# Moving a key and value compression from its own block into the mixers' block of a decoder layer

## The chip, the cores and the metric

One NeuronCore of a Trainium2 chip runs one layer of a hybrid decoder. The metric is the device time of one execution in microseconds (us). TensorE is called PE, VectorE DVE, ScalarE ACT, GpSimd POOL and SyncE SP. Three timed runs of the kernel before stand behind its time, and one profiled execution behind its profile.

## What is computed

x has 2048 rows of 1024 channels. The layer normalises x, multiplies by W_in to get z (3096 columns), runs three groups of heads over z, multiplies the joined result by W_out, adds x, and ends with an MLP. The groups are a retention (4 heads of 64), a short gated convolution, and an attention of 8 heads in 2 key groups with three branches: compressed, selected and window. The change is about what feeds the compressed branch:

```python
def compress(t, pe, w1, w2):
    blocks = kv_heads(t)[:, win_idx] + pe[None, None, :, None, :]
    flat = blocks.transpose(0, 1, 3, 2, 4).reshape(b, n_cmp, G, CMP_LEN * d)
    return jax.nn.silu(flat @ w1) @ w2

k_cmp = rms_norm(compress(k_c, pe_k, w1_k, w2_k), k_gain)
v_cmp = compress(v_c, pe_v, w1_v, w2_v)
```

A window is 32 rows long and starts at every 16th row, so there are 127 of them; d is 64, so flat has 2048 columns and w1 is 2048 x 64. There are two kinds (keys and values) and two groups (G). Nothing of the compressed branch, the first in each tile's attention, can start before k_cmp is there.

## The kernel before

build_layer (L2012) issues five phases. Each is a block of its own: five instruction streams (SP, POOL, ACT, DVE, PE), each in its own fixed order, synchronised by semaphores, and all engines meet at the end of a block.

**projection_phase (L56)** computes z in two halves of 8 row tiles. In each half 9 column blocks of W_in are loaded by SP, split by ACT (split_hi, L160) and POOL into a high and a low part, and multiplied by PE. DVE copies the sums out and SP stores them to z_scratch in DRAM.

**compress_phase (L411)** is the compression. SP loads the identity, then kv, the 256 key and value columns of all 16 row tiles, in one DMA (L480); then it waits until DVE has cleared w1, w2 and pe_rows (L604 to L606), and loads the weights twice, once for each group's half of the partitions (L485 to L487), and then the constants that the mixers need. PE transposes kv in 32 pieces (L549), ACT copies them to kvT (L587). w1 is laid out block-diagonally as 128 x 128 for each of the 32 positions l, so that one matmul serves both groups: kind 0 takes 32 matmuls (L561), each with the 127 columns of kvT that start at l and lie 16 apart. Then the bias of both kinds, pe @ w1, takes 64 matmuls with one moving column (L569), then kind 1 takes its 32 (L561). SiLU is made by ACT and DVE, the second product is at L574, the keys are normalised with a square root on POOL (L536, L537), transposed (L579) and copied to cmp_k (L637). POOL meanwhile fills masks and constants (L503 to L533), and ACT writes the rows that mark the key blocks into ka_s (L590).

**mixers_phase (L758)** starts after that. The class Plan (L666) writes out one list of steps, and PE, ACT and DVE each go through it in this order, doing what is theirs. The list begins with prep(0), the preparation of tile 0 in 22 pieces (PIECES, L645), and goes on with prep(1) merged into the first attention steps. The pieces:

- "squares" (ACT), "sums" (DVE) and "gates" (DVE) read the loaded tile of z;
- "fill qq" to "fill q1" are work of PE into one PSUM bank, prep_ps, and each "read" empties it before the next "fill": qq and kz are transposes (L1298), scores 4 matmuls (L1302), output 12 matmuls (L1308 to L1310), k, q0 and q1 transposes (L1316);
- "normalise k", "normalise q", "high" and "low" are DVE and ACT work on the normalised queries and keys.

POOL has no list. For each tile it copies the values (L964, L967), makes the rotation (L977 to L986, which releases "fill qq"), the root for the normalisation (L993), the convolution taps (L998 to L1004), then waits for the retention's output and finishes it (L1007 to L1013), and only then begins the next tile. SP's load(i) (L914) brings tile i by five DMAs on one semaphore: z, two copies of columns shifted by one and two rows (L928; of tile 0 these have 127 and 126 rows), the rotation (L930) and a selection table (L931). The step "compressed" (L1318) is the first that needs cmp_k, and its first instruction is the mask matmul at L1322. output_phase and mlp_phase follow and are the same in both kernels.

An fp32 matmul of the program appears in the trace as two records, a transpose as one.

Of the kernel before, what the change touches and what calls it, by code (L numbers as in the profile page):

```python
# [24 lines left out]
ALU = mybir.AluOpType  # L25
# [6 lines left out]
P = 128  # L32
BANK = 512
# [22 lines left out]
def projection_phase(nc, x, norm_mix, w_in, identity, z):  # L56
# [17 lines left out]
    with ExitStack() as stack:  # L74
# [7 lines left out]
        sum_sq = m.sb("sum_sq", [P, 2])  # L82
        mean_sq = m.sb("mean_sq", [P, 2])
        rstd = m.sb("rstd", [P, 2])
# [24 lines left out]
        z_free = m.sems("z_free", ZR)  # L109

# [45 lines left out]
        def _(act):  # L156
# [25 lines left out]

            act.sem_inc(product, RING * TT)
            for n in range(XR):
                load_x(n)
            for half in range(HALVES):
                first = half * TT
                square(first)
# [12 lines left out]
                with act.Fori(0, NB // RING - 1) as r:  # L201
                    for u in range(RING):
                        split_hi(r * RING + (half * NB + RING + u), u, r + (half * NB // RING + 1))

        @block.gpsimd
        def _(pool):
            def split_lo(n, u):
# [171 lines left out]
QR = 3  # L379
MAX_ROW = 96  # L380
# [4 lines left out]
class Constants:  # L385
# [3 lines left out]
    def __init__(self, m, S, conv_width):  # L389
        self.ident = m.sb("ident", [P, P])  # L390
        self.ident_bf = m.sb("ident_bf", [P, P], BF16)
        self.ones = m.sb("ones", [P, P], F32R)
# [10 lines left out]
        self.qa_w = m.sb("qa_w", [P, QR, NSA_HEADS, P], F32R)  # L403
        self.qa_s = m.sb("qa_s", [P, QR, NSA_HEADS, P], F32R)
# [4 lines left out]


def compress_phase(nc, z, weights, conv_w, q_gain, k_gain, tables, consts, keys, values):  # L411

    S = z.shape[0]
    NT = S // P
    NBLK = S // SLC_LEN
    NW = (S - CMP_LEN) // STRIDE + 1  # L420
    KINDS = 2

    with ExitStack() as stack:
        m = Space(nc, stack, "cmp")
        ident = consts.ident
        block_rows = m.sb("block_rows", [P, S])
        kv = m.sb("kv", [P, NT, KINDS * P])
        kvT = m.sb("kvT", [P, KINDS, S])
        w1 = m.sb("w1", [P, KINDS, CMP_LEN, P])
        w2 = m.sb("w2", [P, KINDS, P])  # L430
        pe_rows = m.sb("pe_rows", [P, KINDS, GROUPS, HEAD])
        peT = m.sb("peT", [P, KINDS, CMP_LEN])
        bias = m.sb("bias", [P, KINDS])
        gain = consts.k_gains
        pre = m.sb("pre", [P, KINDS, P])
        den = m.sb("den", [P, KINDS, P])
        act_out = m.sb("silu", [P, KINDS, P])
        kc = m.sb("kc", [P, GROUPS, HEAD])
        sq = m.sb("sq", [P, GROUPS, HEAD])
# [100 lines left out]
        def _(pe):  # L540
# [3 lines left out]
            for q in range(KINDS * NT // 4):  # L544
                j, t0 = divmod(4 * q, NT)
                if q == len(banks):
                    pe.wait_ge(copied, 1)
# [1501 lines left out]
```

## Time and profile before

| | us |
|---|---|
| median of 3 runs | 3451.02 (3449.68 to 3454.45) |
| the profiled execution, its time | 3451.55 |
| the profiled execution, its span in the trace | 3449.6 |
| PE busy | 3202.7 (93%) |
| DVE busy | 1435.8 (42%) |
| POOL busy | 1078.3 (31%) |
| ACT busy | 998.3 (29%) |

Times in the trace count from the start of the span. The profiled execution took 1.95 us more than its span. The share of busy time is a mean over all phases: the page's 40 slices of 86 us show PE busy in nine tenths nearly everywhere, with 6 and 7 tenths in the slices that hold the compression and the first tiles of the mixers. A record's duration overlaps that of the next one on PE, so the price of one in a row of many is the row's length divided by its count.

### The profile page before, as it was taken

How to read it: one execution, taken by the hardware profiler on the slowest of the kernel's cores; microseconds unless marked ns; L12 is line 12 of the kernel's file. 1: busy time of each engine (PE TensorE's matmuls, PEld its weight loads, DVE VectorE, ACT ScalarE, POOL GpSimd, SP SyncE). 2: the span in 40 equal slices, each digit the busy share in tenths (PEclk: the TensorE clock that was granted, in tenths of full speed). 3: DMA queues.
4: the chain of work that ended last, by engine and by line, in shares of the span. 5: the costliest groups of instructions: out<-in, count | busy, mean ns of one | idle time of the engine just before them, and what ended most of it. 6: DMA issues, size and time to landing. Idle time of an engine off the chain costs nothing. (4 is left out here: it accounts for less than half of the span.)

```text
span 3449.6 us, 42933 instructions
## 1 busy us (share of the span) xinstructions
PE 3202.7 (93%) x15500; PEld 2516.8 (73%) x15500; DVE 1435.8 (42%) x2615; ACT 998.3 (29%) x1652; POOL 1078.3 (31%) x615
## 2 busy tenths in 40 slices
PE   7999998667888999999979969999999999999999
PEld 7999998644555555555548758888888878888887
DVE  3113111046656666665532133335433533354333
ACT  3012000033434444444430032232222322232221
POOL 3222221043423223222010044444344444444442
PEclk9999999658889999999999979999999999999999
DMA  5223222210101001000023342223322232333321
GB/s 172 97 96 101 97 96 81 67 55 32 64 32 64 33 32 64 32 32 7 13 105 134 117 157 94 93 94 130 102 97 97 95 126 96 97 98 122 97 97 61
DMA packets 164983, 291.21 MB, mean 84 GB/s; under 512 B 19167, under 2 KB 126559, under 8 KB 162780
## 3 DMA queue, kind: packets, MB, share of 16 engines
q1 hardware_dynamic: 160252, 272.79, 23.4%
q10 hardware_dynamic: 4608, 16.78, 1.4%
q8 instruction: 77, 1.26, 0.2%
q14 instruction: 46, 0.38, 0.0%
HBM read 239.01 MB, written 50.53 MB: 84 GB/s over the span
## 5 line engine op out<-in xcount | busy, mean ns | idle before, releaser
L1752 POOL TENSOR_TENSOR mlp_down_lo<-mlp_down_raw,mlp_down_hi 128x2048 fp32r<-128x2048 f32 x64 | 298.5, 4663 | 750.5 <-ACT mlp_down_hi L1791 750.5
L1872 DVE TENSOR_TENSOR mlp_y<-mlp_acc,mlp_y 128x512 f32<-128x512 f32 x512 | 344.5, 688 | 201.4 <-PE mlp_acc L1950 196.5
L1950 PE MATMUL mlp_acc<-mlp_down_hi,mlp_f_hi 128*128 128x512 f32 x1024 | 402.6, 393 | 10.6 <-DVE mlp_y L1872 10.6
L1928 PE MATMUL mlp_up<-mlp_hT_hi,mlp_up_hi 128*128 128x512 f32 x1024 | 399.6, 390 | 2.5 <-DVE mlp_hT_lo L1894 2.5
L1950 PE MATMUL mlp_acc<-mlp_down_hi,mlp_f_lo 128*128 128x512 f32 x1024 | 400.2, 391 | 0.0
L1950 PE MATMUL mlp_acc<-mlp_down_lo,mlp_f_hi 128*128 128x512 f32 x1024 | 400.1, 391 | 0.0
L1928 PE MATMUL mlp_up<-mlp_hT_hi,mlp_up_lo 128*128 128x512 f32 x1024 | 399.4, 390 | 0.0
L1928 PE MATMUL mlp_up<-mlp_hT_lo,mlp_up_hi 128*128 128x512 f32 x1024 | 399.3, 390 | 0.0
L1859 DVE TENSOR_TENSOR mlp_f<-mlp_relu 128x512 f32<-128x512 f32 x128 | 134.4, 1051 | 601.8 <-ACT mlp_relu L1798 601.8
L311 PE MATMUL proj_acc<-proj_w_hi,proj_hT_hi 128*128 128x344 f32 x1152 | 369.9, 321 | 10.9 <-issue 9.8
L311 PE MATMUL proj_acc<-proj_w_hi,proj_hT_lo 128*128 128x344 f32 x1152 | 367.9, 319 | 0.0
L311 PE MATMUL proj_acc<-proj_w_lo,proj_hT_hi 128*128 128x344 f32 x1152 | 367.6, 319 | 0.0
L1747 POOL TENSOR_TENSOR mlp_up_lo<-mlp_up_raw,mlp_up_hi 128x2048 fp32r<-128x2048 f32 x64 | 317.9, 4966 | 41.3 <-ACT mlp_up_hi L1786 41.3
L1106 ACT ACTIVATE mix_probs<-mix_score 128x512 f32<-128x512 f32 x362 | 214.8, 597 | 387.9 <-PE mix_score L1396 281.6
L1424 PE MATMUL mix_selected<-mix_probs,keys_v_s 128*66 128x512 f32 x544 | 288.7, 613 | 0.0
L1791 ACT CAST mlp_down_hi<-mlp_down_raw 128x2048 fp32r<-128x2048 f32 x64 | 122.5, 1913 | 492.9 <-PE mlp_acc L1950 492.9
L1207 DVE TENSOR_REDUCE mix_part_max<-mix_maxima 128x1 f32<-128x512 f32 (+3 forms) x320 | 192.2, 607 | 148.3 <-PE mix_maxima L1353 75.4
L251 DVE COPY proj_z_out<-proj_acc 128x344 f32<-128x344 f32 x144 | 74.2, 516 | 423.0 <-PE proj_acc L311 422.9
L1950 PEld LDWEIGHTS mlp_acc<-mlp_down_hi,mlp_f_hi 128*128 128x128 f32 x1024 | 193.3, 189 | 53.6 <-DVE mlp_y L1872 13.9
L311 PEld LDWEIGHTS proj_acc<-proj_w_hi,proj_hT_hi 128*128 128x128 f32 x1152 | 216.8, 188 | 11.5 <-issue 10.0
L1928 PEld LDWEIGHTS mlp_up<-mlp_hT_hi,mlp_up_hi 128*128 128x128 f32 x1024 | 192.9, 188 | 43.0 <-DVE mlp_hT_lo L1894 2.9
L1950 PEld LDWEIGHTS mlp_acc<-mlp_down_lo,mlp_f_hi 128*128 128x128 f32 x1024 | 193.2, 189 | 40.4
(251 smaller groups left out, 5427.0 us busy)
## 6 DMA issues: line engine op xcount, KB each, us to landing
mlp_up_raw<-in_w_up SPq DMA_DIRECT2D x64, 1024.0 KB, 5.2
mlp_down_raw<-in_w_down SPq DMA_DIRECT2D x64, 1024.0 KB, 4.8
proj_w_raw<-in_w_in SPq DMA_DIRECT2D x18, 1376.0 KB, 6.4
z_scratch<-proj_z_out SPq DMA_DIRECT2D x144, 172.0 KB, 1.9
mix_z<-z_scratch SPq DMA_DIRECT2D x16, 1548.0 KB, 6.9
proj_x_tile<-in_x ACTq DMA_DIRECT2D x16, 512.0 KB, 3.9
mixed_scratch<-mix_mixed SPq DMA_DIRECT2D x16, 512.0 KB, 2.9
out_mixed<-mixed_scratch SPq DMA_DIRECT2D x16, 512.0 KB, 4.1
```

Of the source, the lines that this page charges most:

```text
L251: nc.vector.tensor_copy(z_out[:, s, :], acc[s][:, 0:BW]).then_inc(copied, 1)
L311: mm = nc.tensor.matmul(acc[s][:, 0:BW], a[:, k, rows], w[:, u, k, :], start=k == 0 and a is h_hi and w is w_hi, stop=k == KT - 1 and w is ...
L1106: ins = nc.scalar.activation(probs[:, p % PR, :], score_ps[n % 2][:, :], ACT.Exp)
L1207: nc.vector.tensor_reduce(dst, bank[:, 0:keys], AX_X, ALU.max).then_inc(maxima_read, 1)
L1424: mm = nc.tensor.matmul(bank[0:VROWS, :], v, probs[:, p % PR, :], start=j == tiles[0], stop=j == tiles[-1])
L1747: nc.gpsimd.tensor_tensor(up_lo[:, b, :, :], up_raw[:, :, :], up_hi[:, b, :, :].bitcast(F32), ALU.subtract).then_inc(up_lo_done, 1)
L1752: nc.gpsimd.tensor_tensor(dn_lo[:, b, :, :], dn_raw[:, :, :], dn_hi[:, b, :, :].bitcast(F32), ALU.subtract).then_inc(dn_lo_done, 1)
L1791: nc.scalar.copy(dn_hi[:, b, :, :], dn_raw[:, :, :]).then_inc(dn_hi_done, 1)
L1859: nc.vector.tensor_tensor(f[:, t % 2, :], relu[:, t % 2, :], relu[:, t % 2, :], ALU.mult).then_inc(f_done, 1)
L1872: nc.vector.tensor_tensor(y[:, yb, tt, cols], acc[i % AR][:, :], y[:, yb, tt, cols], ALU.add).then_inc(added, 1)
L1928: mm = nc.tensor.matmul(up_ps[t % 2][:, :], w[:, b, k, cols], h[:, k, :], start=k == 0 and w is up_hi and h is h_hi, stop=k == KT - 1 and ...
L1950: mm = nc.tensor.matmul(acc[i % AR][:, :], a[:, b, k, tt * P:(tt + 1) * P], w[:, b, k, c * BANK:(c + 1) * BANK], start=k == 0 and a is f_h ...
```

## The change

compress_phase is gone; mixers_phase does its work, and Plan begins with a list in which the compression's 15 pieces and tile 0's 22 pieces are interleaved. The weights are loaded in the projection phase. The layout changes too: kvT holds each group apart, with the odd positions in the upper 64 partitions, so that one matmul takes a pair of positions (128 rows) of one group, with 64 weight columns. There are still 32 matmuls for a kind (2 groups x 16 pairs) and 64 for the bias, and w1 needs neither zeros nor a second copy. What ACT copied from one 128 x 512 bank in one instruction is now two copies of 64 x 512 on ACT (group 0) and two on DVE (group 1).

The order of the steps:

```python
order = ("turn 0", "turn 1", "turn 2", "turn 3", "*squares", "turn 4", "turn 5", "*sums", "turn 6",
         "turn 7", "bias", "first 0", "*fill qq", "*read qq", "*normalise k", "*fill kz", "*read kz", "*normalise q",
         "*high", "first 1", "*low", "*gates", "*fill scores", "*read scores", "silu", "*fill output",
         "*read output", "second", "*fill k", "*read k", "normalise", "*fill q0", "*read q0", "pack",
         "*fill q1", "*read q1", "*output sums")
```

The diff, cut to its core:

```diff
 projection_phase, ACT:
+            def load_early():
+                act.wait_ge(early_cleared, 1)
+                act.dma_start(pairs[:, :, :], pair_rows).then_inc(early_in, 16)
+                for j in range(2):
+                    act.dma_start(w1[:, j, :, :], w1_rows[j].rearrange("(a p) e -> p a e", p=P)).then_inc(early_in, 16)
+                    for g in range(2):
+                        rows = slice(g * P // 2, (g + 1) * P // 2)
+                        act.dma_start(w2[rows, j, rows], w2_rows[j]).then_inc(early_in, 16)
...
             for half in range(HALVES):
                 first = half * TT
+                if half == 1:
+                    load_early()
                 square(first)
                 square(first + 1)
                 split_hi(half * NB, 0, half * NB // RING)
 Plan:
-        self.steps = self.prep(0) + merge(first, self.prep(1))
+        self.steps = self.opening() + merge(first, self.prep(1))
 mixers_phase, SP:
                 sp.dma_start(zt[:, b, :], z[rows, :]).then_inc(tile_in[b], 16)
                 if i == 0:
+                    for s in range(2, 4):
+                        load_kv(s)
                     sp.wait_ge(cleared, 1)
...
-            for i in range(3):
-                load(i)
+            sp.dma_start(ident[:, :], tables["identity"]).then_inc(ident_in, 16)
+            load_kv(0)
+            load_kv(1)
+            load(0)
+            for k in range(3):
+                sp.dma_start(conv_taps[:, k, :], conv_w[k].partition_broadcast(P)).then_inc(conv_in, 16)
+            load(1)
+            for g in range(GROUPS):
+                sp.dma_start(cmp_v[:, g, HEAD:], tables["overlap"]).then_inc(overlap_in, 16)
+            load(2)
 mixers_phase, POOL, between the root and the taps of tile 0:
+                if i == 0:
+                    masks()
+                    pool.wait_ge(cmp_squares, 1)
+                    link(nc.gpsimd.tensor_scalar(cmp_mean[:, :], cmp_ssq[:, :], 1.0 / HEAD, EPS, ALU.mult, ALU.add))
+                    nc.gpsimd.tensor_tensor(cmp_rstd[:, :], cmp_mean[:, :], neg_half[:, 0:GROUPS],
+                                            ALU.pow).then_inc(cmp_powered, 1)
+                    pool.wait_ge(conv_in, 48)
 mixers_phase, ACT, the piece "first":
+                        nc.scalar.activation(pre[:, j, 0:NW], front_ps[:, j * P:j * P + NW], ACT.Identity,
+                                             bias=bias[:, j:j + 1]).then_inc(cmp_biased, 1)
+                        act.wait_ge(cmp_biased, j + 1)
+                        nc.scalar.activation(cmp_den[:, j, 0:NW], pre[:, j, 0:NW], ACT.Exp, scale=-1.0)\
+                            .then_inc(cmp_exp, 1)
+                        rows = slice(BLOCK_ROWS, BLOCK_ROWS + NBLK)
+                        nc.scalar.copy(ka_s[rows, j, :].rearrange("b (c k) -> b c k", k=SLC_LEN),
+                                       ident[rows, rows].unsqueeze(2).to_broadcast([NBLK, NBLK, SLC_LEN]))\
+                            .then_inc(blocks_set, 1)
 mixers_phase, DVE, at its start:
+            nc.vector.memset(pack[:, :, :], 0.0)
+            nc.vector.memset(cmp_v[:, :, 0:HEAD], 0.0)
+            link(nc.vector.memset(qa_w[64:, 0:QR - 1, :, :].bitcast(F32), 0.0))
+            link(nc.vector.memset(ka_w[64:, :, :].bitcast(F32), 0.0))
+            link(nc.vector.memset(ka_w[MAX_ROW:MAX_ROW + 1, :, :].bitcast(F32), 1.0))
+            nc.vector.memset(ka_s[MAX_ROW:MAX_ROW + 1, :, :].bitcast(F32), 1.0).then_inc(blocks_set, 1)
 mixers_phase, PE:
+                    if piece == "bias":
+                        for j in range(KINDS):
+                            at = BANK - KINDS + j
+                            for h in range(GROUPS):
+                                for l in range(PAIRS):
+                                    mm = nc.tensor.matmul(prep_ps[h * HEAD:(h + 1) * HEAD, at:at + 1], w1[:, j, l, :],
+                                                          cmp_pe[:, j, l:l + 1], start=l == 0, stop=l == PAIRS - 1)
+                        mm.then_inc(bias_sum, 1)
+                    elif piece.startswith("turn"):
+                        if j == 0:
+                            pe.wait_ge(kv_in[q], 16)
+                        if q >= len(turn_banks):
+                            pe.wait_ge(turn_read_act, q - len(turn_banks) + 1)
+                            pe.wait_ge(turn_read_dve, q - len(turn_banks) + 1)
+                        for t in range(4):
+                            mm = nc.tensor.transpose(turn_banks[q % len(turn_banks)][:, t * P:(t + 1) * P],
+                                                     kv[:, t0 + t, j * P:(j + 1) * P], ident[:, :])
+                    elif piece.startswith("first"):
+                        for h in range(GROUPS):
+                            pe.wait_ge((turn_read_act, turn_read_dve)[h], (j + 1) * TURNS // KINDS)
+                            for l in range(PAIRS):
+                                mm = nc.tensor.matmul(front_ps[h * HEAD:(h + 1) * HEAD, j * P:j * P + NW], w1[:, j, l, :],
+                                                      kvT[:, j, h, 2 * l:2 * l + (NW - 1) * STRIDE + 1:STRIDE],
+                                                      start=l == 0, stop=l == PAIRS - 1)
```

Four smaller DMAs (row_decay, the two gains, decay) move to ACT's queue at the start of the mixers' block. The rows that mark the key blocks come from the identity instead of a table. The pieces "silu", "second", "normalise" and "pack" do what compress_phase did under the same names. "pack" also clears a slot of qa_w on DVE, since the buffers of the compression share their space with slots of qa_s, qa_w and qb that later tiles use.

## Rows read from the trace of the kernel before

**Rows 1.** Windows: stretch, length, busy PE, PEld, DVE, ACT, POOL; granted clock, DMA share, GB/s
```profile
585.70:724.30 138.60, 76.09 (x349) 71.53 (x350) 25.84 (x36) 17.80 (x34) 43.88 (x57) 0.59 0.27 80
724.30:1770.00 1045.70, 952.95 (x4400) 553.99 (x4400) 625.66 (x1503) 456.78 (x1048) 267.57 (x339) 0.94 0.10 37
```

**Rows 2.** Timeline of the compression (start us, length us, engine, what, count, idle before)
```profile
586.13 0.42 SPq L480 DMA_DIRECT2D cmp_kv<-z_scratch  x1
587.50 6.88 DVE L604 MEMSET cmp_w<- 128x8192 f32 x1 [4.13 <-issue]
594.17 6.52 PE L549 MATMUL cmp_bank<-keys_ident,cmp_kv 128*128 128x128 f32 x32 [11.36 <-DMA cmp_kv<-z_scratch]
...
608.84 14.04 PE L561 MATMUL cmp_bank<-cmp_kvT,cmp_w 128*128 128x127 f32 x64
614.00 3.69 ACT L590 CAST keys_ka_s<-cmp_block_rows 32x2048 fp32r<-32x2048 f32 x2 [12.63 <-DMA keys_k_gains<-in_nsa_k_norm]
...
648.81 14.17 PE L561 MATMUL cmp_bank<-cmp_kvT,cmp_w 128*128 128x127 f32 x64
666.34 1.22 PE L574 MATMUL cmp_bank<-cmp_w,cmp_silu 128*127 128x128 f32 x4 [3.36 <-DVE cmp_silu L617]
671.85 0.42 DVE L637 COPY keys_cmp_k<-cmp_bank 128x256 f32<-128x256 f32 x1 [0.78 <-PE cmp_bank L579]
```

**Rows 3.** Timeline of tile 0's preparation and the first attention step
```profile
672.77 0.33 SPq L923 DMA_DIRECT2D mix_z<-z_scratch  x1
691.15 0.63 ACT L1027 ACTIVATE mix_sq<-mix_z 128x512 f32<-128x512 f32 x1 [27.43 <-DMA mix_sel_table<-in_selection]
709.58 0.69 PE L1308 MATMUL mix_prep<-mix_z,mix_ret_scores 128*128 128x64 f32 x2 [5.73 <-DVE mix_ret_scores L1172]
714.33 0.64 PE L1310 MATMUL mix_prep<-mix_z,keys_zk 128*128 128x64 f32 x2
724.27 0.61 PE L1322 MATMUL mix_front<-keys_ident_bf,keys_cmp_mask 128*128 128x512 bf16 x1 [1.64 <-ACT keys_qa_s L1071]
727.63 1.06 PE L1298 MATMUL mix_prep<-keys_ident,mix_qq 128*128 128x128 f32 x4
```

**Rows 4.** Windows of one us: what the DMA engines moved (last two columns: share, GB/s)
```profile
591.00:592.00 1.00, 0.00 (x0) 0.00 (x0) 1.00 (x1) 0.00 (x0) 0.94 (x2) 0.50 1.09 389
679.00:680.00 1.00, 0.00 (x0) 0.00 (x0) 0.00 (x0) 0.00 (x0) 0.00 (x0) 0.50 0.07 25
```

**Rows 5.** DMA issue of the compression's input (count, KB, us to landing)
```profile
cmp_kv<-z_scratch SPq DMA_DIRECT2D x1, 2048.0 KB, 7.9
```

**Rows 6.** Records by line (durations in ns: min/median/max, first and last start in us)
```profile
L569 PEld LDWEIGHTS cmp_bias_ps<-cmp_peT,cmp_w x128: 192/333/334, 622.5 to 648.5; 128*128 128x128 f32 x128
L1424 PEld LDWEIGHTS mix_selected<-mix_probs,keys_v_s x544: 134/138/251, 775.5 to 1764.9; 128*66 128x66 f32 x182
```

**Rows 7.** Timeline of PE in a stretch at full clock, 8 records with 128 contiguous columns
```profile
1134.86 1.05 PE L1326 MATMUL mix_front<-keys_cmp_k,mix_qb 128*128 128x128 f32 x8
```

**Rows 8.** Timeline of POOL: root, taps, end of tile 0, rotation of tile 1, masks
```profile
599.37 1.81 POOL L507 MEMSET keys_cmp_mask<- 128x2048 bf16 x1
605.04 0.29 POOL L532 TENSOR_SCALAR_AFFINE_SELECT keys_ident_bf<-keys_ident_bf 128x128 bf16<-128x128 bf16 x1
669.30 0.72 POOL L537 TENSOR_TENSOR cmp_rstd<-cmp_mean,cmp_neg_half 128x2 f32<-128x2 f32 x1
700.71 1.53 POOL L998 TENSOR_TENSOR mix_taps<-mix_shifted 128x256 f32<-128x256 f32 x2
715.57 0.65 POOL L1007 TENSOR_TENSOR mix_o_sq<-mix_o_ret 128x256 f32<-128x256 f32 x1 [7.53 <-DVE mix_o_ret L1181]
719.51 0.29 POOL L964 COPY keys_v_w<-mix_z 128x128 f32<-128x128 f32 x1
725.47 0.61 POOL L986 TENSOR_TENSOR keys_zk<-keys_kz,keys_row_decay 128x256 f32<-128x256 f32 x1
```

**Rows 9.** Timeline of ACT in the projection, at the place of the early loads
```profile
250.35 2.50 ACT L160 CAST proj_w_hi<-proj_w_raw 128x2752 fp32r<-128x2752 f32 x1 [25.12 <-DMA proj_w_raw<-in_w_in]
```

More of the change, by code:

```diff
@@ L379 @@
 QR = 3
+PR = 6
 MAX_ROW = 96
@@ L647 @@
           "fill q0", "read q0", "fill q1", "read q1", "output sums")
+CMP_PIECES = tuple(f"turn {q}" for q in range(8)) + ("bias", "first 0", "first 1", "silu", "second", "normalise",
+                                                                  "pack")
 FILLS = [piece[5:] for piece in PIECES if piece.startswith("fill")]
@@ L813, in mixers_phase @@
         gates = m.sb("gates", [P, QR, 3 * NSA_HEADS])
-        taps = m.sb("taps", [P, 3, CW])
         sq = m.sb("sq", [P, NSA_HEADS + 2 * GROUPS, HEAD])
@@ L1283, in _ @@
                 qr = i % QR
+                if kind == "cmp":
+                    piece = step[2]
+                    if piece == "bias":
+                        for j in range(KINDS):
[5 more added lines that the diff above has]
+                        mm.then_inc(bias_sum, 1)
+                    elif piece.startswith("turn"):
+                        q = int(piece[5:])
+                        j, t0 = divmod(4 * q, NT)
+                        if j == 0:
[6 more added lines that the diff above has]
+                                                     kv[:, t0 + t, j * P:(j + 1) * P], ident[:, :])
+                        mm.then_inc(turned, 1)
+                    elif piece.startswith("first"):
+                        j = int(piece[6:])
+                        for h in range(GROUPS):
[4 more added lines that the diff above has]
+                                                      start=l == 0, stop=l == PAIRS - 1)
+                        mm.then_inc(first_sum, 1)
+                    elif piece == "second":
+                        pe.wait_ge(silu_set, 1)
+                        for j in range(KINDS):
+                            mm = nc.tensor.matmul(score_ps[0][0:NW, j * P:(j + 1) * P], silu[:, j, 0:NW], w2[:, j, :],
+                                                  start=True, stop=True)
+                        mm.then_inc(second_sum, 1)
+                    elif piece == "pack":
+                        pe.wait_ge(packed, 1)
+                        for h in range(GROUPS):
+                            mm = nc.tensor.transpose(score_ps[1][:, h * P:(h + 1) * P], pack[:, h, :], ident[:, :])
+                        mm.then_inc(pack_turned, 1)
+                    continue
```

430 lines of the change are left out of this document (194 added, 236 removed).

## The prediction

> **What bounds the kernel now.** I read the windows by stage first. Between the end of the projection and the first instruction of the attention lie 138.6 us in which PE has records in flight for only 76.1 us, at a mean granted clock of 0.59; in the 1045.7 us of mixers behind them PE is busy for 953.0 at 0.94 [rows 1]. So the stretch that the change rebuilds is a chain and not a full engine, and what follows it is a nearly full PE: time taken from the chain should reach the end. The timeline of that stretch shows two chains one behind the other. The compression: the input lands and PE begins at 594.17, the transposes take 6.52 us, the weights come so late that the first product begins only at 608.84, kind 0 takes 14.04, the bias follows up to 648.5, kind 1 takes 14.17, cmp_k is written at 671.85 [rows 2, 6]. Then the mixers' block: tile 0 is asked for at 672.77 and used at 691.15, the attention's mask matmul runs at 724.27 [rows 3]. Nothing in the second chain but that last step needs the first.
>
> **The input.** SP now issues the identity and two quarters of kv, tile 0's z, and the other two quarters: 64 + 2048 + 1548 KB, 3.75 MB. Before, identity and kv (2.16 MB) took 7.9 us from the issue [rows 5], of which 5.6 are bytes at the 389 GB/s of [rows 4] and 2.3 fixed. So the last quarter lands 9.6 + 2.3 = 11.9 us after 586.1, at 598.0. DVE's clearing moves ahead of its first copy: some 8,300 elements by 0.84 ns (6.88 us for 8192), 7 us from 587.5, so to 594.6, hidden under the quarters; uncovered, it would cost its 7 us.
>
> **Tile 0.** It took 18.4 us from the issue [rows 3], with a stretch at 25 GB/s, a sixteenth of 389 [rows 4]: one DMA engine at work alone, which fits the shifted copy of 127 rows. That engine now has 2048/16 = 128 KB of kv ahead, 5.3 us at 25 GB/s: tile 0 is there at 586.9 + 18.4 + 5.3 = 610.6. "squares" stands before "turn 4" on ACT, so four turns wait until then; PE doesn't need them before "first 1". Covered, as below, by bias and first 0.
>
> **PE's list.** With its columns the list is a sum.
> - Transposes: 6.52 us for 32 is 0.204 each [rows 2]; turns 2 to 7 are 24, 4.9 us from 598.0: bias begins at 602.9.
> - Bias: 128 records as before, whose starts lie between 622.5 and 648.5 [rows 6], 0.205 apart, with 128 weight columns. Now there are 64. No row has 64 columns beside one moving column. One end is 0.205 (no gain), the other half of it, 0.102. Loads of 128 and 66 columns at the slow clock last 333 and 251 ns [rows 6], 1.32 ns a column; 64 fewer are 0.085 us less, 0.120 a record. I take this slope, as 66 columns are nearest to 64: 15.4 us, to 618.3, between 13.1 and 26.2.
> - First 0: 64 records, 14.04 us before, 0.22 each [rows 2]; 64 again. Contiguous columns at full clock go at (1.05 - 0.27)/7 = 0.11 [rows 7], while these went at 0.22 whatever the clock, so I lay their price on the moving side, read 16 elements apart, which stays. Taken: 14.1, to 632.4; the other end is 7.
> - ACT's "first" (two small activations, 0.7 us, and one block copy of 1.85, half of 3.69 [rows 2]) comes before "read qq" and holds it; then read qq, 512 columns of ACT like the 0.63 of [rows 3], and fill kz, 1.1 like the 1.06 of 727.63 [rows 3]: with the hand-overs 4.5 us. First 1 begins at 636.9 and ends at 651.0.
> - Fill scores 1.05 (8 records [rows 7]; 2.1 slow), its reading 0.7, then the rest of the preparation: before, from the output's first record to the mask matmul, 724.27 - 709.58 = 14.7 [rows 3]. Its 24 records took 5.4 at the slow clock; straight behind 14 us of products I expect full clock and 2.9. Second and pack squeeze in for 1.0. Sum 1.05 + 0.7 + 14.7 - 2.5 + 1.0 = 15.0: the mask matmul at 666.0, against 724.27: 58.3 us earlier (slow clock: 3.5 less).
>
> On the weight load the trace leaves a slope and a constant. The Trainium skill, "TensorE: Matmul & The Clock Gate", section "LDWEIGHTS (loading the stationary operand)", has its time in proportion to the columns, with no constant; by it bias would take the 13.1 us of the low end, and the forecast would be 2.3 us lower. The rows side with the slope, since 66 columns cost three quarters of 128 and not half.
>
> **What is late next: POOL.** POOL has tile 0's rotation and root, then masks (6.0 us, 599.37 to 605.33), then waits for the squares of the compressed keys, and taps, output and all of tile 1 are queued behind that wait. Rotation, root and masks end at about 626, in time. Fill output ends at 655.6; from the second product to the end of POOL's root went 670.0 - 666.3 = 3.7 [rows 2, 8]: 659.3. Then taps, 7.3 (700.71 to 7.53 before 715.57); from the output's squaring to the next tile 3.9; from there to the end of the rotation 6.6 [rows 8]. Sum: 677.1. Before, POOL had done the taps while it waited for the output, and tile 1's rotation was ready at 726.1, 1.5 us before PE used it at 727.63. Now PE would want it at 666.0 + 3.4 = 669.4 and stands until 677.1: 7.7 us given back, since PE's order puts the rest of the attention behind it. Net 727.6 - 677.1 = 50.5 us.
>
> **Costed at nothing.** Seven DMA issues of at most 1.5 us each on ACT, before the squares of tile 8, lie in 25.12 us in which ACT waits for weights [rows 9]; without that cover they would cost up to 10 us. Their 1.1 MB ride beside a DMA share of 0.31. The old weight loads, the table, a block's end: gone with the chain they stood in. Conv taps, tile 1, overlap: landed long before 650.
>
> **Sum.** The profiled execution took 3451.55 us, 0.53 over the median; less 50.5 that is 3401.0, and by the median 3400.5, the forecast.
>
> **Rivals.**
> - **Bias at its old price** (0.205): PE's records might have a floor that columns don't touch; for it speaks that N = 1 went no faster than transposes. 10.8 us dearer: 3411.3.
> - **Products get cheaper too**: if the weight load, not the stride, held them at 0.22, both kinds go at 0.11, 14 us less: 3386.4. Against it: the rate didn't change when the clock doubled.
> - **POOL's lateness is absorbed**: DVE has "gates" and maxima to do meanwhile, and later waits shrink; 58.3 saved: 3392.7.
> - **It doesn't overlap as written**: bias waits in truth for tile 0 (a late quarter of kv behind z), so it begins at 611: 8 us dearer, 3408.6.
> - **Slower**: a matmul that writes only half of the array's columns and then the other half might cost double. The place is PE's 256 records of bias and first products; at 0.41 and 0.44, twice the old prices, bias is 37 us and the products 28 us above the forecast's, and 65 less 50.5 makes it 14.5 us slower than before: 3465.5. It decides from 0.2 us a record more than I took. Against it: 66 weight columns load in less time than 128 [rows 6]. The Trainium skill, "TensorEngine Tiling (Array Packing)", section "Tiling Modes", says that a change of tiling mode drains the engine; here the mode would change only at the few borders between groups, and no run here shows the price.
>
> **The numbers.** Forecast's own case 0.50, bias at its old price 0.14, absorbed 0.12, cheaper products 0.10, no overlap 0.07, slower 0.03, and 0.04 for mishaps that leave little. Two tenths left out, the range goes from 3387 (products nearly at the low price) to 3414 (bias old, clock slow). A measurement here tells 0.2%, 7 us, from no change. Faster 0.94, within 0.02, slower 0.04.
>
> **What would show it.** In the changed profile: bias at about 603 and its 128 records in 15 us; first products 14 us each; tile 0's squares at 611; the mask matmul near 666; a wait of PE's fill qq of tile 1 for POOL of some 7 us; the stretch from projection to attention down from 138.6 to about 80; the mixers behind it, and the projection, unchanged within 3 us. I am wrong if the bias takes 26 us, if the first products change, if PE doesn't wait for POOL there, or if the rest of the mixers gets longer by what the opening gained.

## The result and the profile after

The change makes the kernel **faster by 57.3 us**: 3393.1 us in the median of four runs (3389.7 to 3400.5) against 3450.4 (3449.7 to 3454.5), a ratio of 0.9834 (95% interval 0.9817 to 0.9852). The forecast was 3400.5 in a range of 3387 to 3414. The profiled execution took 3393.48 us against 3451.55, 58.1 less, and it is the one whose rows stand here.

The windows by stage first: the stretch from the projection to the first attention step, and as many microseconds of mixers behind it as it takes (columns as in [rows 1]).

```profile
585.70:660.80 75.10, 54.10 (x347) 44.03 (x348) 34.48 (x53) 22.40 (x42) 23.31 (x36) 0.70 0.30 98
660.80:1712.00 1051.20, 953.61 (x4400) 553.83 (x4400) 624.56 (x1500) 457.37 (x1048) 275.64 (x351) 0.94 0.11 37
```

The opening fell from 138.6 to 75.1 us, PE's busy time in it from 76.1 to 54.1: two thirds of what went was waiting. The mixers behind it have the same 953 us of PE work as in [rows 1], but are 5.5 us longer, which is nearly the wait on POOL below. The projection kept its length: the mixers' block begins within 0.2 us of where compress_phase began (SP's first issue at 585.89 against 585.73).

PE's timeline through the opening (start, length, engine, line, what, count, idle before it and what ended it):

```profile
592.99 1.08 PE L1293 MATMUL mix_score<-keys_ident,cmp_kv 128*128 128x128 f32 x4 [10.01 <-DMA cmp_kv<-z_scratch]
602.05 1.12 PE L1293 MATMUL mix_maxima<-keys_ident,cmp_kv 128*128 128x128 f32 x4 [0.27 <-DMA cmp_kv<-z_scratch]
606.21 9.82 PE L1281 MATMUL mix_prep<-cmp_pe_pairs,cmp_w 128*64 128x1 f32 x125
616.29 12.70 PE L1301 MATMUL mix_front<-cmp_kvT,cmp_w 128*64 128x127 f32 x62
628.91 0.66 PE L1333 MATMUL mix_prep<-keys_ident,mix_qq 128*128 128x128 f32 x4
632.95 13.15 PE L1301 MATMUL mix_front<-cmp_kvT,cmp_w 128*64 128x127 f32 x64
646.03 1.16 PE L1337 MATMUL mix_prep<-mix_qqT,mix_kzT 128*128 128x128 f32 x8
660.78 0.61 PE L1362 MATMUL mix_front<-keys_ident_bf,keys_cmp_mask 128*128 128x512 bf16 x1 [1.64 <-ACT mix_qa_s L1004]
672.01 1.09 PE L1333 MATMUL mix_prep<-keys_ident,mix_qq 128*128 128x128 f32 x4 [7.67 <-POOL keys_zk L881]
```

The input's quarters come one by one (592.99, 602.05); bias, kind 0, tile 0's first fill, kind 1 and the rest of the preparation then follow with gaps of at most 2.8 us, where [rows 2, 3] had the weights' lateness and a whole second load. The mask matmul is at 660.78, 63.5 us earlier than in [rows 3]. The last row is what was given back: fill qq of tile 1 waits 7.67 us for POOL and starts at 672.01, 55.6 earlier than the 727.63 of [rows 3].

POOL's own timeline shows why.

```profile
653.67 0.19 POOL L894 TENSOR_SCALAR mix_cmp_mean<-mix_cmp_ssq 128x2 f32<-128x2 f32 x1 [26.79 <-DVE mix_cmp_ssq L1093]
...
671.26 0.61 POOL L881 TENSOR_TENSOR keys_zk<-keys_kz,keys_row_decay 128x256 f32<-128x256 f32 x1
```

After tile 0's root and the masks POOL stands 26.8 us, until 653.67, for the squares of the compressed keys; taps, output and tile 1's rotation all come behind, and keys_zk ends at 671.87, when PE starts. In [rows 8] POOL had the taps done before the output asked.

Three rows of the timeline from other engines: ACT at the early loads in the projection, where the wait of [rows 9] is 21.00 instead of 25.12 us, so the issues, which end at 227.4, fitted into it; SP's issue of tile 0's shifted rows, which stalls for 11.3 us; and the squares of tile 0 on ACT.

```profile
250.68 2.50 ACT L161 CAST proj_w_hi<-proj_w_raw 128x2752 fp32r<-128x2752 f32 x1 [21.00 <-DMA proj_w_raw<-in_w_in]
...
590.09 11.28 SPq L785 DMA_DIRECT2D mix_shifted<-z_scratch  x2
...
611.50 0.63 ACT L960 ACTIVATE mix_sq<-mix_z 128x512 f32<-128x512 f32 x1 [6.85 <-DMA mix_sel_table<-in_selection]
```

The attention's mask matmul of the second unit came at 742.48 before and comes at 686.98 now, the third at 768.71 and 713.15: 55.5 and 55.6 us. What POOL took wasn't won back there. The other 2.5 us to 58.1 come later and are within what runs of one kernel differ by: the way from the second mask matmul to the third alone took 26.2 us here and 23.3 and 27.8 in two other traces of the same kernel.

### The profile page after: what moved, and what is told of

Read it like the earlier page. It is cut to its first block and busy times, and to the rows that moved or that the text cites. A ratio compares the mean times of both kernels' runs of the same rounds, so it can differ in the third digit from the quotient of the medians.

```text
span 3391.7 us, 42938 instructions
## 1 busy us (share of the span) xinstructions
PE 3179.0 (94%) x15498; PEld 2487.8 (73%) x15498; DVE 1443.5 (43%) x2633; ACT 1003.8 (30%) x1660; POOL 1065.3 (31%) x607
## 5 line engine op out<-in xcount | busy, mean ns | idle before, releaser
L1039 ACT ACTIVATE keys_probs<-mix_score 128x512 f32<-128x512 f32 x362 | 214.8, 598 | 387.3 <-PE mix_score L1436 282.6
L1464 PE MATMUL mix_selected<-keys_probs,keys_v_s 128*66 128x512 f32 x544 | 288.8, 614 | 0.0
```

What stands on the lines that cost most here:

```text
L1039: ins = nc.scalar.activation(probs[:, p % PR, :], score_ps[n % 2][:, :], ACT.Exp)
L1464: mm = nc.tensor.matmul(bank[0:VROWS, :], v, probs[:, p % PR, :], start=j == tiles[0], stop=j == tiles[-1])
```

## The experiments

Eleven runs were made, of nine edited kernels and twice of the changed kernel as it is. They fall in three groups, each beside fresh runs of the kernel before on the same chip (3451.8, 3452.2 and 3451.1 us in the median). Every edit is on the changed kernel. As the medians of one kernel scatter (the changed one alone gave 3396.95 and 3394.18, single runs from 3388.7 to 3400.0), the place of a named instruction in the trace is the sharper measure, and both are given. Places count from the start of the span; the mixers' block begins between 585.5 and 586.2 in all these traces but one, the run with the bias in front, where it begins at 587.22. Differences of medians are against 3396.95 in the first two groups (the changed kernel ran beside the first) and against 3394.18 in the third. The groups are: the changed kernel, taps, bias in front and one behind the other; late weights, twice the columns, grouped by pair and three edits; only the large weights late, the changed kernel again and all four.

**The changed kernel again, twice.** No edit.

> The changed kernel as it is, on the same chip as the next three, to compare them with. All theories: 3390 to 3396 us, the stages where they were: mask matmul of the attention at 660.8, a wait of PE for POOL of 7.7 us before tile 1's fill qq.

Measured: 3396.95 us (3395.2 to 3399.7), ratio 0.9843 (0.9827 to 0.9860).

> The changed kernel itself on the chip of this batch, to set the others against: 3393 to 3397.

Measured: 3394.18 us (3388.65 to 3399.95), ratio 0.9839 (0.9818 to 0.9861). The gain repeats. In the trace of the first of the two the mask matmul is at 660.13 and fill qq of tile 1 at 671.75, behind 8.06 us for POOL; the runs below are held against these two marks.

**Taps lead on POOL.** The root of the compressed keys moves behind tile 0's taps, which now only wait for the first products (a release in POOL's list that comes at the right time).

```diff
 if i == 0:
-    pool.wait_ge(cmp_squares, 1)
-    ... root of the compressed keys ...
+    pool.wait_ge(first_sum, KINDS)
 ... taps of tile 0 ...
+if i == 0:
+    pool.wait_ge(cmp_squares, 1)
+    ... root of the compressed keys ...
```

> Edit: of tile 0, POOL makes the convolution taps as soon as the second kind's products are done, and waits for the compressed keys' squares only behind them. Theory (POOL's lateness goes through to the end): the taps' 6.7 us leave the chain of tile 1, PE's wait of 7.7 us for POOL falls to about 1, and the time falls by 5 to 7 us against the changed kernel. Rival (the lateness is absorbed by later waits): the wait of PE vanishes too, but the time falls by less than 2 us.

The timeline of POOL and PE in this run:

```profile
646.14 1.53 POOL L897 TENSOR_TENSOR mix_taps<-mix_shifted 128x256 f32<-128x256 f32 x2 [19.15 <-PE mix_front L1303]
...
659.38 0.20 POOL L913 TENSOR_SCALAR mix_o_mean<-mix_o_ssq 128x4 f32<-128x4 f32 x1 [3.81 <-DVE mix_o_ssq L1180]
668.85 1.09 PE L1335 MATMUL mix_prep<-keys_ident,mix_qq 128*128 128x128 f32 x4 [4.25 <-POOL keys_zk L881]
```

Measured: 3391.20 us, ratio 0.9826 (0.9810 to 0.9843), 5.7 under the changed kernel's median; the intervals overlap. The taps run from 646.14, and POOL reaches the root at 653.99, within 0.7 us of its place in the changed kernel's traces (653.67 and 653.38). PE's wait for POOL falls from 8.06 to 4.25 us, not to 1 (the row at 659.38: POOL now waits 3.81 us for DVE's sum over the output), and fill qq of tile 1 comes 2.9 us earlier. So **POOL's order is what held PE there**, for about half of the 8 us; in the other half POOL waits for the output itself. The mark gives 2.9 us; the rest of the 5.7 is not separated from scatter.

**Bias leads on PE.** Only the hand-written order is changed, "bias" ahead of "turn 0".

```diff
-CMP_PIECES = tuple(f"turn {q}" for q in range(8)) + ("bias", "first 0", ...
+CMP_PIECES = ("bias",) + tuple(f"turn {q}" for q in range(8)) + ("first 0", ...
```

> Edit: PE takes the bias before the first turn and no longer behind the eighth. Theory (the opening is one chain through PE from the last kv quarter on): bias hides under the loads from 589 to 599, the first products begin at about 607 instead of 615.8, the mask matmul comes at about 652, and the time falls by 7 to 9 us. Rival (tile 0's arrival at 611.5 and POOL's rotation and root behind it take over): the mask matmul comes no earlier than 657 and the time falls by 4 us at most. Second rival (DVE and ACT, which get turn 0 six us later, become late): no gain.

SP's first issue and PE's timeline, and the window of the bias (columns as in [rows 1]):

```profile
587.22 0.35 SPq L795 DMA_DIRECT2D keys_ident<-in_identity  x1
...
590.18 12.61 PE L1281 MATMUL mix_prep<-cmp_pe_pairs,cmp_w 128*64 128x1 f32 x128 [5.87 <-POOL mix_selection L823]
653.65 0.61 PE L1362 MATMUL mix_front<-keys_ident_bf,keys_cmp_mask 128*128 128x512 bf16 x1 [1.64 <-ACT mix_qa_s L1004]
665.27 1.08 PE L1333 MATMUL mix_prep<-keys_ident,mix_qq 128*128 128x128 f32 x4 [8.06 <-POOL keys_zk L881]
```

```profile
590.20:602.80 12.60, 12.60 (x129) 12.59 (x130) 5.30 (x3) 0.00 (x0) 0.26 (x2) 0.50 0.84 307
```

Measured: 3385.43 us (3379.1 to 3388.4), ratio 0.9810 (0.9794 to 0.9826), 11.5 below the changed kernel; the mask matmul comes 6.5 us earlier, and so does fill qq of tile 1. But the block itself begins 1.5 us later in this trace (587.22 against 585.75 in the changed kernel's), by the projection's scatter, so within the block both marks come 8.0 us earlier. The medians differ by 3.5 us more than that. In the traces, the stretch from 660 to 1000 us had a granted clock of 0.85 here and of 0.81 in the changed kernel's, and the profiled execution here is the fastest of its four (3379.12); single runs of one kernel lie 11 us and more apart. The bias fills the time in which PE otherwise waits for the input. The transposes lead in the changed kernel, and that order costs it 8 us. All 128 records ran here at a granted clock of 0.50, the low level: 12.61 us, 0.098 a record.

**The two chains one behind the other.** The list puts all of the compression ahead of tile 0's pieces; early weights, early tile load and the single block stay. Kind 1's product goes to another bank, and POOL makes the root of the compressed keys ahead of tile 0's.

> Edit: one block still, loads as in the change, but all 15 pieces of the compression stand before the 22 of tile 0's preparation; kind 1's product goes to another bank, and POOL makes the compressed keys' root before tile 0's. Theory (the change gains by laying two chains of waits beside each other): compression ends near 650, the preparation takes its 33 us behind it, the mask matmul comes at 680 to 688 and the time rises by 20 to 27 us against the changed kernel, so that about 35 of its 57 us remain. Rival (the gain is from the removed block, the early loads and the cheaper bias, since PE has the same records to run in either order): the time rises by less than 8 us.

PE's timeline at the marks:

```profile
677.95 0.61 PE L1360 MATMUL mix_front<-keys_ident_bf,keys_cmp_mask 128*128 128x512 bf16 x1 [1.64 <-ACT mix_qa_s L1001]
681.31 1.06 PE L1331 MATMUL mix_prep<-keys_ident,mix_qq 128*128 128x128 f32 x4
696.18 0.59 PE L1360 MATMUL mix_front<-keys_ident_bf,keys_cmp_mask 128*128 128x512 bf16 x1 [0.94 <-DVE mix_qa_s L1204]
```

Measured: 3404.49 us (3400.3 to 3406.4), ratio 0.9861 (0.9844 to 0.9877): 7.5 us slower than the changed kernel, not 20 to 27. My expectation failed. At the mask matmul the loss is 17.8 us (677.95 against 660.13), but here POOL has nothing late: fill qq of tile 1 follows without a wait at 681.31, 9.6 us behind the changed kernel's, and the second unit's mask matmul is 9.5 behind (696.18 against 686.73). What interleaving saves at the first mark, it gives back by half to POOL. **Interleaving itself is the smaller part of the gain.**

**Weights late.** The seven loads go back from the projection to the start of the mixers' block, on ACT's queue.

```diff
-                if half == 1:
-                    load_early()
...
+            act.dma_start(cmp_pe[:, :, :], pair_rows).then_inc(late_in, 16)
+            for j in range(2):
+                act.dma_start(w1[:, j, :, :], ...).then_inc(late_in, 16)
+                for g in range(2):
+                    act.dma_start(w2[rows, j, rows], w2_rows[j]).then_inc(late_in, 16)
...
 PE, the piece "bias":
+pe.wait_ge(late_in, 16 * 7)
```

> The compression's weights (7 transfers, 1.1 MB) are issued on ACT's queue at the start of the mixers' block instead of during the projection; nothing else differs. Theory: they run beside kv and tile 0's z at a queue already full (about 390 GB/s for 4 MB), so kv's last quarter lands 3 us later, the bias waits for its weights until about 608 to 612 instead of 606, and the issues hold ACT 5 to 9 us, which delays its copies of the turns; mask matmul at 663 to 668, the time 3 to 8 us above the changed kernel's 3397. Rival: the loads hide behind the wait for kv altogether, and the time is within 2 us of it. Other rival: they come as late as before the change, 10 us and more behind, and the time is 3405 to 3410.

The timeline of ACT, with its issues, and of PE:

```profile
589.93 9.51 ACTq L917 DMA_DIRECT2D cmp_w<-in_cmp_w_k  x2
600.11 12.37 ACTq L917 DMA_DIRECT2D cmp_w<-in_cmp_w_v  x2
612.52 0.58 ACT L927 COPY cmp_kvT<-mix_score 64x512 f32<-64x512 f32 x1 [109.50 <-issue]
...
623.53 12.29 PE L1276 MATMUL mix_prep<-cmp_pe_pairs,cmp_w 128*64 128x1 f32 x125 [7.48 <-DMA cmp_w<-in_cmp_w_v]
680.58 0.61 PE L1357 MATMUL mix_front<-keys_ident_bf,keys_cmp_mask 128*128 128x512 bf16 x1 [1.63 <-ACT mix_qa_s L998]
```

Measured: 3416.54 us (3405.2 to 3419.9), ratio 0.9887 (0.9868 to 0.9906): 19.6 us above the changed kernel, the mask matmul 20.5 later. All three theories had the time too low. ACT stands 9.5 and 12.4 us at the issues of the small loads, the copies of the turns begin only at 612.52, and the bias, which waits for all seven loads, begins at 623.53.

**Only the large weights late.** As before, but the small loads stay in the projection, so that ACT issues nothing behind the large ones. The bias of both kinds waits for both.

> Only the two 512 KB loads of the first products' weights move to ACT's queue at the start of the mixers' block; the bias table and the four small loads of the second product's weights stay in the projection. When all seven moved, the mask matmul came 20 us later and ACT stood 9.5 and 12.4 us at the issues of the small loads. If what was paid there were those issues (ACT held, its copies of the turns late), then without them ACT begins its copies before 596, the bias begins at 606 to 612, the mask matmul at 662 to 667 and the time is 3399 to 3404. If it was the bytes that came late, the bias begins again near 623, the mask matmul near 680, and the time is 3414 to 3418.

The same timeline, and then the DMA issues (count, KB each, median us to landing), two of this stretch and last one of the changed kernel's projection:

```profile
588.69 9.63 ACTq L926 DMA_DIRECT2D cmp_w<-in_cmp_w_v  x1
598.36 0.58 ACT L936 COPY cmp_kvT<-mix_score 64x512 f32<-64x512 f32 x1 [95.38 <-issue]
...
620.75 12.29 PE L1285 MATMUL mix_prep<-cmp_pe_pairs,cmp_w 128*64 128x1 f32 x125 [13.59 <-DMA cmp_w<-in_cmp_w_v]
677.39 0.61 PE L1366 MATMUL mix_front<-keys_ident_bf,keys_cmp_mask 128*128 128x512 bf16 x1 [1.64 <-ACT mix_qa_s L1007]
```

```profile
cmp_w<-in_cmp_w_k ACTq DMA_DIRECT2D x1, 512.0 KB, 17.0
cmp_w<-in_cmp_w_v ACTq DMA_DIRECT2D x1, 512.0 KB, 32.0
...
cmp_w<-in_cmp_w_k ACTq DMA_DIRECT2D x1, 512.0 KB, 4.6
```

Measured: 3411.35 us (3406.4 to 3420.8), ratio 0.9895 (0.9865 to 0.9924); 17.2 above the changed kernel, and less than the 3414 to 3418 that this theory had; mask matmul at 677.39. The first theory fell: ACT's copies start 14 us earlier, at 598.36, but the bias still waits until 620.75. **It was the late landing of the large loads**: they took 17.0 and 32.0 us from their issue beside kv and z; in the projection one of them took 4.6. Freeing ACT was worth 3 us of the 20. What the late landing costs hangs on the wait, too. The keys' weights were issued at 587.66 and so were there at 604.7; only the values' came at 620.7. With a wait for each kind, kind 0 could have begun some 14 us sooner, an estimate from these landings; no run tried it. Whether the bytes, the order of the queues or the size of the rows made the loads slow wasn't separated either.

**Twice the weight columns under the bias.** The 128 records load two pairs' weights side by side, 128 columns instead of 64; the bias comes out as other sums.

```diff
-mm = nc.tensor.matmul(prep_ps[h * HEAD:(h + 1) * HEAD, at:at + 1], w1[:, j, l, :],
+mm = nc.tensor.matmul(prep_ps[:, at:at + 1],
+                      w1[:, j, l // 2 * 2:l // 2 * 2 + 2, :].rearrange("p a e -> p (a e)"),
```

> The 128 records of the bias load 128 weight columns (two pairs' side by side) instead of 64 and write 128 partitions; the bias itself comes out as other sums, everything else is as in the changed kernel. If the price of such a record is set by the weight columns, it goes from 0.078 to 0.15 to 0.21 us, the bias takes 19 to 26 us instead of 9.8, and the mask matmul comes 9 to 16 us later, near 672, the time near 3409. If it is a price per record, the bias stays near 10 us and the time at 3396. In between, near 0.12, would be the slope and constant of the forecast read from the other end.

PE's timeline; then the part of the bias that ran at the low clock, once as a window for the clock and once as a timeline for the count:

```profile
604.74 24.80 PE L1281 MATMUL mix_prep<-cmp_pe_pairs,cmp_w 128*128 128x1 f32 x128
674.04 0.61 PE L1363 MATMUL mix_front<-keys_ident_bf,keys_cmp_mask 128*128 128x512 bf16 x1 [1.63 <-ACT mix_qa_s L1004]
```

```profile
609.00:628.50 19.50, 19.50 (x93) 19.50 (x93) 3.63 (x5) 5.86 (x12) 13.76 (x19) 0.50 0.28 105
...
608.71 19.98 PE L1281 MATMUL mix_prep<-cmp_pe_pairs,cmp_w 128*128 128x1 f32 x93
```

Measured: 3409.03 us (two runs), ratio 0.9876 (0.9856 to 0.9896); the mask matmul 13.9 us later. The bias takes 24.80 us, 0.194 a record at a mean clock of 0.56. At a granted clock of 0.50 alone, 93 records start over 19.98 us less the last one's 0.35, 0.213 a record, against 0.098 with 64 columns at 0.50 in the run in which the bias leads. **Twice the columns, a little over twice the price: no constant.**

**Keys and values grouped by pair.** kvT is stored so that the 127 windows of one pair are neighbours; the copies out of the banks take 256 columns each instead of 512.

```diff
-kvT = e.sb("kvT", [P, KINDS, GROUPS, S])
+kvT = e.sb("kvT", [P, KINDS, GROUPS, STRIDE // 2, S // STRIDE])
...
-nc.vector.tensor_copy(kvT[0:HEAD, j, 1, t0 * P:(t0 + 4) * P], bank[HEAD:, :])
+by_pair = bank[HEAD:, :].rearrange("p (c a two) -> p two a c", a=STRIDE // 2, two=2)
+nc.vector.tensor_copy(kvT[0:HEAD, j, 1, :, c0:c1], by_pair[:, 0])
...
-kvT[:, j, h, 2 * l:2 * l + (NW - 1) * STRIDE + 1:STRIDE],
+kvT[:, j, h, l % 8, l // 8:l // 8 + NW],
```

> The transposed keys and values are stored by pair of tokens, so that every moving operand of the first products is 127 neighbouring columns instead of 127 columns 16 elements apart; the copies out of the transposes' banks move 256 columns each instead of 512, read 2 to 16 apart. If the stride holds the products at 0.205 us a record (the forecast's reading), they go at 0.11 to 0.13, 7 to 8 us for 64 instead of 13.1, the mask matmul comes near 650 instead of 660.1, and the kernel is 9 to 12 us faster than the changed one, near 3386. If the weight load or the four-byte data holds them, they stay at 0.19 to 0.21, the mask matmul moves by less than 2 us, and the time is 3395 to 3398.

PE's timeline; then two windows of this run for the clock, and the records of the same stretches (neighbouring columns); then two stretches of the kernel before (16 elements apart), the first at a granted clock of 0.50, the second at 1.00:

```profile
629.37 7.76 PE L1301 MATMUL mix_front<-cmp_kvT,cmp_w 128*64 128x127 f32 x64
651.41 0.61 PE L1362 MATMUL mix_front<-keys_ident_bf,keys_cmp_mask 128*128 128x512 bf16 x1 [1.64 <-ACT mix_qa_s L1004]
```

```profile
615.80:618.80 3.00, 3.00 (x17) 3.00 (x16) 0.16 (x1) 0.08 (x1) 2.60 (x6) 0.50 0.03 11
621.80:624.80 3.00, 3.00 (x30) 2.90 (x27) 1.76 (x3) 0.00 (x0) 2.59 (x5) 1.00 0.00 0
...
615.59 3.38 PE L1301 MATMUL mix_front<-cmp_kvT,cmp_w 128*64 128x127 f32 x15
621.58 3.36 PE L1301 MATMUL mix_front<-cmp_kvT,cmp_w 128*64 128x127 f32 x30
```

```profile
608.84 3.00 PE L561 MATMUL cmp_bank<-cmp_kvT,cmp_w 128*128 128x127 f32 x13
614.69 5.59 PE L561 MATMUL cmp_bank<-cmp_kvT,cmp_w 128*128 128x127 f32 x25
```

Measured: 3385.90 us (3376.3 to 3390.5), ratio 0.9800 (0.9781 to 0.9819), 11 us below the changed kernel; the mask matmul at 651.41, 8.7 earlier. Kind 1 takes 7.76 us instead of 13.15, 0.121 a record, its first 1.7 us at the low clock. A single record lasts 0.42 us at the low clock and 0.27 at the full one (0.39 at both when strided), and overlaps the next; a row's length less this, shared among the records before the last, gives the price of one. Contiguous, it is 0.21 us at the low clock (2.96 / 14) and 0.107 at the full one (3.09 / 29); strided, 0.22 at either (2.61 / 12 and 5.20 / 24). The forecast's reading held: **the stride sets the price** at full clock, where it doubles it; at the low clock it costs next to nothing.

**Three edits together**: taps lead, bias leads, and the first rows of tile 0's shifted copies go in a transfer of their own, so that the large one has 112 rows instead of 127 or 126.

```diff
-cut = s if i == 0 else 0
+cut = 16 if i == 0 else 0
+if i == 0:
+    sp.dma_start(shifted[s:16, b, s - 1, :], z[0:16 - s, CC:CC + 2 * CW]).then_inc(shift_in, 16)
```

> The taps lead on POOL and the bias leads on PE, both as in the runs that tried one of them, and the shifted copies of tile 0 are split so that 112 rows go in one transfer and the 15 or 14 others in another. If the two savings add up (5.7 and 11.5 us by the medians, 3 and 6.5 by the matmul of tile 1's scores), the time is 3380 to 3386; if they share one wait, so that only the larger counts, 3385 to 3388. Split rows: in place of a stretch at 25 GB/s the DMA engines share the shifted copy, SP's stall of 11.3 us at that issue falls below 4, tile 0's squares begin 2 to 5 us earlier than 612.96; that buys nothing by itself, since PE is busy with the products until 622.

The timeline of SP's issues, ACT and PE:

```profile
589.92 5.85 SPq L787 DMA_DIRECT2D mix_shifted<-z_scratch  x1
...
604.49 0.66 PE L1299 MATMUL mix_maxima<-keys_ident,cmp_kv 128*128 128x128 f32 x4 [0.54 <-DMA cmp_kv<-z_scratch]
...
607.22 0.61 ACT L966 ACTIVATE mix_sq<-mix_z 128x512 f32<-128x512 f32 x1
...
651.64 0.61 PE L1368 MATMUL mix_front<-keys_ident_bf,keys_cmp_mask 128*128 128x512 bf16 x1 [1.64 <-ACT mix_qa_s L1010]
659.96 1.09 PE L1339 MATMUL mix_prep<-keys_ident,mix_qq 128*128 128x128 f32 x4 [4.76 <-POOL keys_zk L884]
```

Measured: 3384.58 us (3383.7 to 3390.9), ratio 0.9810 (0.9794 to 0.9826). The marks add up: the mask matmul is 8.5 earlier than the changed kernel's (8.0 for the bias in front), fill qq of tile 1 11.8 (8.0 and 2.9 for the taps). By the medians it is no better than the run in which the bias leads alone. SP's 11.3 us at the issue fell to 5.9, not below 4, and the squares of tile 0 moved from 611.50 to 607.22, where they follow ACT's copies without a wait. The wait for kv's last quarter now ends only at 604.49 instead of 602.05, presumably since the rows that were moved share the engines with it. PE waits only 0.54 us for it.

**All four together**, the best version found.

> Taps lead on POOL, bias leads on PE, tile 0's shifted copies split, keys and values grouped by pair so that the first products read neighbouring columns. Theory: the two products save 4 to 5 us each over the run with the other three (mask matmul at 651.64 there), so the mask matmul comes at 642 to 644, PE then waits 4 to 6 us for POOL at tile 1's fill as there, tile 1's scores begin at 650 to 653, and the time is 3374 to 3379. Rival: POOL's own chain (tile 0's root, the compressed keys' root, the output, tile 1's rotation) doesn't move up with the products, PE's wait at tile 1's fill grows to 8 us or more, and the time is 3380 to 3384.

PE's timeline:

```profile
607.23 6.77 PE L1307 MATMUL mix_front<-cmp_kvT,cmp_w 128*64 128x127 f32 x64
638.36 0.61 PE L1368 MATMUL mix_front<-keys_ident_bf,keys_cmp_mask 128*128 128x512 bf16 x1 [1.63 <-ACT mix_qa_s L1010]
647.25 1.09 PE L1339 MATMUL mix_prep<-keys_ident,mix_qq 128*128 128x128 f32 x4 [5.33 <-POOL keys_zk L884]
```

Measured: **3371.11 us** (3369.5 to 3375.2), ratio 0.9779 (0.9758 to 0.9800). Beside it on the same chip the changed kernel took 3394.18, so this is 23.1 us (0.7%) below it, with no run of one among those of the other. The products take 6.77 us each (0.106 a record, at full clock) and not the 8 to 9 I had expected, the mask matmul is at 638.36, PE's wait for POOL 5.33 us.

## Why the prediction was right, and which terms were off

The rival cases and the forecast differ by single terms; here is each by its own step.

- **The chain gives way to the end**: right. The measured time is all but that of the rival "POOL's lateness is absorbed" (3392.7), and yet PE did wait for POOL: the number came near by other terms, a shorter bias above all. That the time landed 7 us under the forecast and inside the range is in part errors that cancel, as the next points show. 63.5 us at the mask matmul against 58.3 forecast, 55.6 against 50.5 at tile 1's fill, 57.3 by the medians.
- **The input**: the last quarter at 598.0 was too early. The waits for it end at 600.66 and 602.05, and the bias began at 606.21, not 602.9. What was off is the division of 3.75 MB by the 389 GB/s of [rows 4] right from the issue; the windows show the engines below that at first, 118 GB/s from 588 to 590 and 313 in the two microseconds after. What held them there isn't shown.
- **The bias: the mis-sized term.** 15.4 us was forecast, between 13.1 and 26.2; it took 9.9 (125 records in 9.82), below the low end. I had laid a straight line through the lengths of two weight loads in [rows 6], which leaves a constant of half the longer one (164 of 333 ns), and so took only 0.085 us off the 0.205. The run with 128 columns shows no constant: 0.213 against 0.098 us, both at the low clock. And weight loads overlap: in the records by line of the changed kernel they last 227 ns in the median (min/median/max), while 128 of them start in 9.8 us.

```profile
L1281 PEld LDWEIGHTS mix_prep<-cmp_pe_pairs,cmp_w x128: 133/227/231, 606.2 to 616.0; 128*64 128x64 f32 x128
```

  The rule that I had set against the line is the right one: the Trainium skill, "TensorE: Matmul & The Clock Gate", section "LDWEIGHTS (loading the stationary operand)", has the time in proportion to the columns, and the traces agree, within a tenth: 0.098 us for 64 and 0.213 for 128 at the low clock. By it the forecast had 13.1 us, and where the whole bias ran at the low clock it took 12.6. That it took 9.9 here is the clock, of which a mean of 0.66 was granted between 606 and 616: 52 records run from 606.21 to 609.2 at the full level, 56 from 610.08 to 615.7 at the low one.
- **The first products**: 14.1 us forecast for each, 12.8 and 13.1 measured (0.20 a record). That the stride holds them was argued; the run grouped by pair shows it. "Products get cheaper too" was right only in that a layout can do it, not this change.
- **From first 0 to the mask matmul**: hand-over 4.0 us against 4.5, the rest of the preparation 14.75 against 15.0. The 5.2 us by which the mask matmul came early are 3.3 late in the input, 5.5 less for the bias, 2.3 less for both products, and 0.7 in the rest.
- **Tile 0**: squares at 611.50 against 610.6, by the reading of one engine at work alone; with the rows split they are at 607.22. DVE's clearing ended at 595.4 against 594.6 and was hidden, as forecast.
- **POOL**: a wait of 7.7 us forecast, 7.67 measured, though each end of it lay 5 us off. "POOL's lateness is absorbed" is wrong: the second and third mask matmuls are 55.5 and 55.6 us earlier, as is the fill. With the taps in front half of the wait goes. The mixers behind the mask matmul were to stay within 3 us and are 5.5 longer: the forecast had put POOL's wait into them and left it out of that sign.
- **Costed at nothing**: the issues in the projection cost nothing, as forecast. But the loads' own worth was never a term of the sum, since it went under "gone with the chain": it is 20 us against loads that land late and are all waited for at once, the largest single part that a run measured; beside it interleaving is worth 7.5, and 64 weight columns instead of 128 some 14 of the bias.
- **Slower** and **bias at its old price**: nothing of either. 64-column matmuls that write one half of the array's columns and then the other cost half of the 128-column ones in the bias, and in the first products no more than these (0.20 against 0.22 us). The Trainium skill, "TensorEngine Tiling (Array Packing)", section "Tiling Modes", has a drain at a change of mode; in this trace, where records of 128 and of 64 weight columns follow each other (606.21, 628.91 and 646.03 above), each row starts before the modelled end of the one in front of it, and no gap is to be seen.

What stays open: how the remaining 57.3 - 20 - 7.5 - 14 = 16 us divide between the block that fell away, the tile loaded early, the input in quarters and the copies shared by ACT and DVE; the parts need not add up, and none of these was undone alone. The gap between medians and marks (3.5 us for the bias in front) was not resolved either.

## What to carry to other kernels

Move the weights' loads to where the queues are idle before reordering anything: here that was worth more than the interleaving of the two chains. Where they can't move, let each product wait for its own (an estimate above, not tried here). When two chains are laid beside each other, follow each engine's own list to the first wait that now stands ahead of work which it used to do in its idle time; that wait (POOL's, 7.7 us) can be read out of the trace beforehand. Put the work that needs no input first, and lay data out so that what a matmul reads is contiguous: the two, with the taps in front and the split rows, brought another 23 us.

## What was not expected of the hardware

- **A moving operand read 16 elements apart costs the same at both levels of the clock, a contiguous one doesn't.** 127 columns, apart: 0.20 to 0.22 us at 1.2 and at 2.4 GHz. Contiguous: 0.21 at 1.2 and 0.106 at 2.4.
- **A load shared with a full queue took up to seven times as long.** 512 KB of weights: 4.6 us in the projection, 17.0 and 32.0 beside kv and z, where SP's transfers held most of the engines' time.
- **An issue can hold its engine for ten microseconds.** ACT for 9.6 us at one issue of 512 KB behind another (588.69 above), SP for 11.3 us at the shifted rows; in both cases transfers issued earlier were still under way.
- **The clock stayed low under a busy PE.** PE had stood 5.9 us before the bias in front; through the 12.6 us of back-to-back records that follow, the granted clock was 0.50, its lower level of 1.2 GHz.
